# S5 output products of a hybrid decoder step: four state tiles at a time in place of two

## What is computed

```python
# 32 groups of 16 channels, 64 complex states each
x_re = einsum('gsc,blgc->blgs', bb_re, u)          # input products
x_im = einsum('gsc,blgc->blgs', bb_im, u)
h_re, h_im = scan over time of h = ab * h + x      # complex, diagonal
y = einsum('gcs,blgs->blgc', c_re, h_re) - einsum('gcs,blgs->blgc', c_im, h_im)   # output products
y = y + d_skip * u
out = glu(gelu(y) @ w_glu)
```

## Time and profile before

| | |
|---|---|
| median of three timed runs | 725.71 us (722.58 to 727.33) |
| the profiled execution's own time | 725.09 us |
| its span, first to last instruction | 723.3 us |
| PE busy over the span | 649.7 us (90%) |
| DVE, ACT, POOL busy | 375.3, 137.4, 115.9 us |
| mean granted PE clock | 0.943 |

### The profile page before, as it was taken

How to read it: one execution, slowest core, us unless ns; L and a number is a source line. 1 busy time by engine, 2 the same in 40 slices (tenths; PEclk the granted TensorE clock), 3 DMA queues, 4 the chain that set the end, 5 groups by cost and what they waited for, 6 DMA issues and landing times. The chain is left out here.

```text
span 723.3 us, 8946 instructions
## 1 busy us (share of the span) xinstructions
PE 649.7 (90%) x3371; PEld 401.4 (55%) x3371; DVE 375.3 (52%) x1018; ACT 137.4 (19%) x280; POOL 115.9 (16%) x181
## 2 busy tenths in 40 slices
PE   4989599599999989999988999839999999998994
PEld 2467478376767768666656777622344344343342
DVE  1479999587789913467775221650142243131135
ACT  3231122400100033222230000501110111110103
POOL 1000000087899403100300000000000000000000
PEclk9999799699999999999999999758999999999997
DMA  8989314102333370099938333969999999999941
GB/s 274 381 220 389 140 54 156 33 15 102 117 117 116 117 240 3 2 387 346 368 94 259 116 130 117 394 275 392 430 422 429 423 428 425 424 426 427 428 191 68
DMA packets 64382, 178.58 MB, mean 247 GB/s; under 512 B 9828, under 2 KB 27956, under 8 KB 58192
## 3 DMA queue, kind: packets, MB, share of 16 engines
q1 hardware_dynamic: 56628, 168.48, 60.7%
q10 hardware_dynamic: 6412, 4.77, 2.3%
q0 software_dynamic: 1296, 4.72, 1.7%
HBM read 170.56 MB, written 7.39 MB: 246 GB/s over the span
## 5 line engine op out<-in xcount | busy, mean ns | idle before, releaser
L595 PE MATMUL psum<-projection_region,ring 128*128 128x288 f32 x768 | 200.0, 420 | 13.5 <-ACT projection_region L1168 7.7
L595 PEld LDWEIGHTS psum<-projection_region,ring 128*128 128x128 f32 x768 | 148.6, 196 | 61.9 <-issue 20.6
L595 PE MATMUL psum<-ring,gate_region 128*64 128x512 f32 x400 | 106.8, 604 | 2.4 <-DMA mixer_region<-in_w 1.7
L1457 DVE TENSOR_TENSOR gate_region<-gate_region,psum 128x288 f32<-128x288 f32 (+1 forms) x16 | 12.0, 750 | 171.7 <-PE psum L595 149.4
L1168 ACT ACTIVATE gate_region<-psum 128x512 f32<-128x512 f32 (+2 forms) x65 | 35.8, 564 | 278.6 <-PE psum L595 170.2
L595 PE MATMUL psum<-mixer_region,gate_region 128*64 128x512 f32 x256 | 77.8, 593 | 0.0
L595 PEld LDWEIGHTS psum<-ring,gate_region 128*64 128x64 f32 x400 | 33.7, 139 | 69.6 <-issue 68.4
L1463 DVE SCALAR_TENSOR_TENSOR x_features<-psum,modulation,x_features 128x256 f32<-128x256 f32 x72 | 34.1, 473 | 29.3 <-PE psum L595 29.1
L579 POOL TENSOR_TENSOR gate_region<-group_key 128x1 f32<-128x1 f32 x8 | 1.6, 206 | 254.5 <-DVE gate_region L1989 145.3
L595 PEld LDWEIGHTS psum<-mixer_region,gate_region 128*64 128x64 f32 x256 | 24.2, 137 | 22.1 <-issue 21.7
L1457 DVE TENSOR_TENSOR projection_region<-psum,mixer_region 128x256 f32<-128x256 f32 x64 | 27.1, 423 | 17.5 <-PE psum L595 13.0
(11 more groups left out here) (248 smaller groups left out, 829.9 us busy)
## 6 DMA issues: line engine op xcount, KB each, us to landing
ring<-in_w SPq DMA_DIRECT2D x25, 2048.0 KB, 21.4
mixer_region<-in_w SPq DMA_DIRECT2D x15, 2048.0 KB, 26.1
ring<-in_w_ada SPq DMA_DIRECT2D x12, 2048.0 KB, 9.5
ring<-in_w_in SPq DMA_DIRECT2D x10, 2048.0 KB, 10.4
projection_region<-in_w SPq DMA_DIRECT2D x4, 2048.0 KB, 22.7
tok_region<-in_w SPq DMA_DIRECT2D x4, 1536.0 KB, 25.1
ring<-in_w_glu SPq DMA_DIRECT2D x2, 2048.0 KB, 8.2
ring<-in_w_out_a SPq DMA_DIRECT2D x2, 2048.0 KB, 10.2
```

Of the source, the lines that this page charges most:

```text
L595: return nc.tensor.matmul(out, lhsT, rhs, start=first, stop=last, skip_group_check=True)
L1457: return v.tensor_tensor(out, x, y, op)
```

## The change

`s5_out` now takes the four tiles 4a to 4a+3: it waits for all four, makes the four real products in column groups 0, 1, 2, 3, and then the four imaginary ones in the same round. The four calls stand ahead of projection tiles n = 7, 12, 17 and 22, the first three directly ahead of the input products of pairs 3, 5 and 7. The number of matmuls, their shapes, and the programs of DVE, POOL, ACT and SP are the same.

```diff
-            def s5_out(p):
-                a_ = p // 2
-                pe.wait_ge(s5_h, 2 * p + 2)
-                if p % 2 == 0 and a_ >= 2:
+            def s5_out(a_):
+                pe.wait_ge(s5_h, 4 * a_ + 4)
+                if a_ >= 2:
                     pe.wait_ge(s5_yev, a_ - 1)
                 for q in range(2):
-                    for i in (2 * p, 2 * p + 1):
+                    for i in range(4 * a_, 4 * a_ + 4):
                         r = 32 * (i % 4)
                         last = mm(ps[r:r + 32, 6 + a_ % 2, 0:TP], cTs5[:, q, a_, r:r + 32], h5[:, 2 * (i % 4) + q, :], q == 0, q == 1)
                         if q == 1:
...
             S5P = S5T // 2
             in_at = {(5 * p) // 2: p for p in range(S5P)}
-            out_at = {20: S5P - 2, 22: S5P - 1}
+            out_at = {7: 0, 12: 1, 17: 2, 22: 3}
             for t in range(T_Z, NT):
                 n = t - T_Z
+                if n in out_at:
+                    s5_out(out_at[n])
                 if n in in_at:
-                    if in_at[n] >= 2:
-                        s5_out(in_at[n] - 2)
                     s5_in(in_at[n])
-                elif n in out_at:
-                    s5_out(out_at[n])
                 tile(t)
```

## The result

Over 20 runs each the changed kernel takes 732.73 us (median) and the kernel before 727.05. The ratio is 1.0069, with a 95% interval of 1.0043 to 1.0094: about 5 us slower. Two further comparisons of the same pair gave 1.0111 (1.0073 to 1.0149) and 1.0057 (1.0026 to 1.0089). It is slower in all three, by 0.6 to 1.1%; the forecast was 2.8 us slower. Ratios and their intervals leave out runs more than 1.5% above the fastest of their kernel, which the medians keep; the profiled execution of the change (738.96 us) is one of those left out, so what follows leans on two further profiles of it as well (730.49 and 732.14 us).

A forecast was written before the change was run, and what follows sets the result against it. PE was taken to bound the loop; it saves 3.7 us of work but waits start the sample's products 2.9 us later, rounded to +2.8: 725.09 + 2.8 = 727.9 us. The eight-in-ten range was 724.3 to 731.5.

The forecast's parts named there:

- What bounds the kernel: From 140 to 256.5 us PE bounds the kernel, busy for 114.96 of 116.5 us, POOL and DVE close behind.
- the 3.7 that PE saves: Output products in the loop: 7.9 us before, four calls at 4.2 us after, so PE saves 3.7 us of work.
- The cap of 2.6 us: At the loop's end: the recurrence ends at 253.9 us, so at most 2.6 us of 256.5 could come out.
- The call's price of 1.06 us: Each new output call on PE has 16 records, four per column group as before, and takes 1.06 us.
- The chain of waits: POOL begins tile 4 3.4 us late, PE waits 1.7 us at n = 10, sample's products start 2.9 us later.
- I count no fall: PE's new waits, 1.7 us and less, cause no fall of the clock; each fall would cost 1.7 us.
- Rival 3: PE's clock falls at two of the longer waits: 731.3 us; chance 0.08.
- The base: The forecast adds to the profiled execution's own 725.09 us, 0.6 us under the median of the three runs.
- rival 1: POOL keeps its faster 5.41 us per tile throughout: 2 to 2.5 us off the sum, 725.5 us; chance 0.18.
- rival 2: The loop ends with the recurrence at 253.9 us, 2.6 us earlier: 722.5 us; chance 0.06.
- rival 4: The four column groups do not run side by side, each output call takes 2.1 us: 732.1 us; chance 0.04.

## Why the prediction was right in direction and short in size

- **What bounds the kernel:** right, PE does: with more buffers the stretch fell by 3.6 us, the 3.7 that PE saves by the sum. The cap of 2.6 us was wrong. The chain that ends with the recurrence ran earlier too, to 87.35 us behind the start of n = 5, where before it was 89.54.
- **The call's price of 1.06 us:** right, 1.07. The reason given was incomplete: going round the groups isn't needed for it.
- **The chain of waits:** right, step by step, in the first profile (its times less 2.81 us). POOL's tile 4 at 174.70 (174.6 was forecast), PE's wait at n = 10 of 1.69 us (1.7), the second call at 199.16 (199.2), POOL's tile 8 at 200.33 (200.3). After that it parts: tile 12 at 228.48, not 226.0, behind a wait of 0.73 us at n = 12 that was not forecast and the slow tile at n = 15. In the other two profiles the wait at n = 10 is longer than forecast, 2.12 and 2.04 us. Less 1.7 us for each fall the three profiles give 2.8 to 3.0 us for the stretch; 2.9 was forecast, and the kernel with the filled waits, which has no fall, measured 3.5.
- **"I count no fall":** this is the step that failed, a term of the sum set to nothing. The new waits of PE at n = 10 and 15 made the clock fall once, twice and twice in the three profiles, 1.7 us each, 2.8 us on average; filled with work, they made none. The forecast had rested on one wait of 2.00 us that passed without a fall; in the change one of 1.69 passed, those of 1.89, 2.04, 2.12 and twice 2.16 did not. One harmless wait was no ground for a price of zero. The Trainium skill's page "TensorE: Matmul & The Clock Gate" (section "Why this matters for your kernels") warns of idle gaps between bursts, but of longer ones than any of these. The prediction left that out; by that section's words no fall was due here, and the measurement decides otherwise. Rival 3, the clock falling at two waits, is what happened; 0.08 for it was far too little.
- **The base:** the forecast started from an execution of 725.09 us; 20 runs of the kernel before gave 727.05. So of the 4.8 us by which 732.73 lies above the forecast of 727.9, the base makes 2.0 and the falls, at their average, 2.8. That this adds up so well is partly luck, with ratios that mean 4.1 to 8.1 us in three comparisons of the same pair. The range ended at 731.5: it took in rival 3 (731.3) on the lower base, but not on this one. Nor is 1% the least that can be told from no change: the interval of the result is 0.25% to either side.
- **Rivals 1, 2 and 4** fall: POOL took 5.90 us for a tile beside DVE (182.73 to 188.63 in the change, not shown), the saving stayed away until there were more buffers, and the groups do run side by side. The terms of rival 1 add up to as much as 3.1 us, not 2.5; the forecast does not use them.

Open: in the two controls with extra work at n = 20, and in the kernel before with more buffers, the ratio is 1.6 to 2.9 us above what the stretch shows. In single profiles the way from the sample products to the output projection, where these kernels have the same code, took 123.8 us at a mean granted clock of 0.96 (the kernel before with more buffers) and 133.9 us at 0.89 (fourteen extra matmuls at n = 20; neither shown). One profile of a kernel therefore cannot tell whether a later start costs more than its length, and how much of the change's 4.1 to 8.1 us lies behind the loop stays open.

## What to carry to other kernels

When work that frees a buffer is gathered into fewer, larger calls, the first part of it is done later: work out when the buffer comes free and who waits for it, before counting what the call saves. Here one projection tile of place decided between 5 us lost and nothing, and buffers taken from a dead table brought the saving out. With buffers to spare the larger calls are worth their 3.6 us. A new wait on a TensorE that was busy throughout should be priced with a possible fall of its clock, not with its length alone: here five of six waits of 1.69 to 2.16 us had one, of 1.7 us each. Useless matmuls in their place kept the clock in the stretch, though the whole time gained little that could be measured.

## What was not expected of the hardware

Two calls that use column groups 0, 1 and 2, 3, issued one behind the other, overlap as fully as one call that goes round all four: 16 records in 1.08 and 1.07 us, where each call by itself takes 1.06 for 8. So what the change gained on PE came from standing together, and the new order of the groups had no part in it.

A fall of the clock needs no wait right ahead of it. Behind the loop the second GLU product (16 records) took 5.84 us with more buffers, at 262.73 with no wait shown (granted clock 0.50 from 264.73 to 266.73), and 4.15 us before, behind a wait of 0.42 us. What decided there was not tested.
